# Delta-rule scan of a two-block model: raw key products of a chunk made once for both directions, with a new operation order on four engines

## The reference, cut to what matters

```
kb = k * beta;  gamma = exp(G_i - G_j) below the diagonal
a_low = strict_lower(kb k^T * gamma)          # per chunk and direction
(u, w) = (1 + a_low)^-1 [v*beta, kb*exp(G)]
qk = (q k^T) * gamma
v_new = u - w s;  o = (q exp(G)) s + qk v_new;  s = s exp(G_last) + (k exp(G_last - G))^T v_new
```

## Time and profile before

| | |
|---|---|
| median of 3 runs | 3566.6 us (3563.71 to 3573.29) |
| the profiled execution, its own time | 3574.62 us |
| its span, first to last instruction | 3572.8 us |
| PE busy, share of the span | 3451.9 us, 97% |
| DVE, ACT, POOL busy | 61%, 27%, 13% |
| scan stage, first and second half of the heads | from 1580.5 and from 1919.7 us, some 209 us each |

### The profile page before, as it was taken

One profiled execution on the slowest core, in us unless ns is written; L12 is line 12 of the kernel. 1 busy time (PEld: TensorE's weight loads), 2 busy tenths in 40 slices (PEclk: granted clock), 3 DMA queues, 4 the chain that ended last, 5 costly groups with the idle time before them and its releaser, 6 DMA issues.

```text
span 3572.8 us, 59170 instructions
## 1 busy us (share of the span) xinstructions
PE 3451.9 (97%) x24990; PEld 2877.7 (81%) x24990; DVE 2172.1 (61%) x3040; ACT 980.9 (27%) x1835; POOL 473.9 (13%) x400
## 2 busy tenths in 40 slices
PE   8999999999999999999999999999999999999998
PEld 6777887877778888879887887799988786668887
DVE  4655777646557776655565556854475653864347
ACT  1243101222430012433343322443322203720011
POOL 0000000000000000015402440034440001502000
PEclk9999999999999999999999999999999999999999
DMA  4311444323015443210010013032252331022222
GB/s 173 111 37 48 185 189 176 137 100 112 25 50 207 188 166 125 104 37 3 3 65 25 3 48 125 36 114 100 106 194 71 104 116 48 1 72 104 95 95 95
DMA packets 58055, 338.93 MB, mean 95 GB/s; under 512 B 7580, under 2 KB 8092, under 8 KB 23240
## 3 DMA queue, kind: packets, MB, share of 16 engines
q1 hardware_dynamic: 30492, 220.50, 16.9%
q10 hardware_dynamic: 27308, 114.71, 8.8%
HBM read 309.64 MB, written 18.21 MB: 92 GB/s over the span
## 4 chain that ended last, share of the span: by engine, by line
PE 76%; DVE 8%; PEld 6%; DMA 3%; issue 3%; ACT 2%; PEldq 1%; POOL 0%; POOLq 0%; ACTq 0%; DVEq 0%; another core or an unknown queue 0%; SPq 0%
PE psum L567 19%; PE psum L569 18%; PE psum L568 18%; PE psum L2650 4%; PE psum L2657 4%; DMA pieces_in<-pieces 2%; PEld psum L567 2%; PEld psum L569 2%; PEld psum L568 2%; PE psum L1412 1%; PE psum L1396 1%; PE psum L1385 1%; PE psum L2789 1%; PEldq L507 1%; PE psum L4234 1%
## 5 line engine op out<-in xcount | busy, mean ns | idle before, releaser
L569 PE MATMUL psum<-xt_operands,pieces_lo 128*128 128x512 f32 (+1 forms) x2016 | 748.9, 371 | 0.0
L567 PE MATMUL psum<-xt_operands,pieces_hi 128*128 128x512 f32 (+1 forms) x1840 | 700.2, 381 | 16.3 <-DVE xt_operands L826 7.0
L568 PE MATMUL psum<-xt_operands,pieces_hi 128*128 128x512 f32 (+1 forms) x1840 | 689.7, 375 | 0.0
L567 PE MATMUL psum<-pieces_hi,xt_operands 128*128 128x512 f32 x1276 | 508.9, 399 | 18.5 <-DVE pieces_lo L616 9.4
L568 PE MATMUL psum<-pieces_lo,xt_operands 128*128 128x512 f32 x1320 | 517.6, 392 | 0.0
L569 PE MATMUL psum<-pieces_hi,xt_operands 128*128 128x512 f32 x1276 | 500.6, 392 | 0.0
L569 PEld LDWEIGHTS psum<-xt_operands,pieces_lo 128*128 128x128 f32 x2016 | 379.6, 188 | 62.7
L567 PEld LDWEIGHTS psum<-xt_operands,pieces_hi 128*128 128x128 f32 x1840 | 346.9, 189 | 87.6 <-issue 13.6
L568 PEld LDWEIGHTS psum<-xt_operands,pieces_hi 128*128 128x128 f32 x1840 | 347.2, 189 | 59.2
L583 DVE CAST pieces_hi<-pieces_in 128x2048 fp32r<-128x2048 f32 x165 | 208.2, 1262 | 254.5 <-DMA pieces_in<-pieces 125.2
L567 PEld LDWEIGHTS psum<-pieces_hi,xt_operands 128*128 128x128 f32 x1276 | 242.3, 190 | 76.4 <-DVE pieces_lo L616 10.5
(11 more groups left out here) (464 smaller groups left out, 5586.6 us busy)
## 6 DMA issues: line engine op xcount, KB each, us to landing
pieces_in<-pieces SPq DMA_DIRECT2D x210, 1024.0 KB, 4.9
x_mem<-ada ACTq DMA_DIRECT2D x28, 1024.0 KB, 4.8
arena<-ada ACTq DMA_DIRECT2D x20, 1024.0 KB, 4.8
hid<-arena ACTq DMA_DIRECT2D x22, 384.0 KB, 4.4
arena<-mods ACTq DMA_DIRECT2D x10, 512.0 KB, 17.0
arena<-hid ACTq DMA_DIRECT2D x3, 1536.0 KB, 11.6
arena<-arena ACTq DMA_DIRECT2D x32, 128.0 KB, 4.4
arena<-hid ACTq DMA_DIRECT2D x1, 3840.0 KB, 16.2
```

The costliest lines, as they stand in the source:

```text
L567: signal_later(k, pe.matmul(out, sh, mh, start=start, stop=False, skip_group_check=reopened))
L568: signal_later(k, pe.matmul(out, sh, ml, start=False, stop=False, skip_group_check=reopened))
L569: return pe.matmul(out, sl, mh, start=False, stop=stop, skip_group_check=reopened)
```

## The change

Raw products are made once. `kk` and `qk` run only at the first visit of a chunk (`first_visit`). There DVE reads them from PSUM as before, and ACT then copies them to SBUF (new `kkc`, `qkc`, 128x512 each) into places that are free at that time (`kept`): parts of `oacc`, of kT and qT, and of k and v for the context chunks. At the second visit DVE's `low0` and `qg` read the kept copy, so that both of their inputs are in SBUF.

The bank of a raw product comes free only when ACT has copied it. `oa` of a first visit is a copy in place of an addition, so that `oacc` is no longer cleared; the two clears of the state no longer wait for one another.

All four orders are new, and PE and DVE work on steps t-1 and t-2 (`LAG` is 2, one more turn of the loop). Several waits that followed from the old order are written out (among them `dup` before the next `diff`, `-xx1`, `-wy`); where the order of signals implies them, no wait is issued.

```diff
+def first_visit(s, d):
+    return CHUNKS[d][s] not in CHUNKS[1 - d][:s]
+def kept(k, name, s, d):
+    c, q = CHUNKS[d][s], int(name == "qk")
+    if c >= NT1:
+        return k.oacc[:, 2 * (c - NT1) + q, :, :]
+    if c in (0, 3):
+        return (k.kT if c == 0 else k.qT)[:, :, P * (NT1 + q):P * (NT1 + q) + P]
+    return (k.kc_ if c == 1 else k.vc_)[:, NT1 + q, :, :]
...
-TAKEN = dict(gb="diff", kk="low0", qk="qg", ...
+TAKEN = dict(gb="diff", kk="kkc", qk="qkc", ...
...
     def kk(s, d):
+        if not runs(s) or not first_visit(s, d):
+            return
         product(s, d, "kk", chunk(k.kT), chunk(k.kT))
...
-    for t in range(N_STEPS + 1):
-        a3(t - 1, 0); x4(t - 1, 0); a1(t - 1, 1); x8(t - 1, 0); ks(t - 1, 1); wy(t - 1, 0); x2(t - 1, 1)
-        a2(t - 1, 1); qk(t - 1, 1); xx0(t - 1, 0); a3(t - 1, 1); z0(t - 1, 0); x4(t - 1, 1); y1(t - 1, 0)
-        o1(t - 1, 1); x8(t - 1, 1); xx1(t - 1, 0); gb(t, 0); wy(t - 1, 1); w2(t - 1, 0); y2(t - 1, 0); gb(t, 1)
-        xx0(t - 1, 1); xx2(t - 1, 0); z0(t - 1, 1); y1(t - 1, 1); vn(t - 1, 0); xx1(t - 1, 1); o1(t - 1, 0)
-        w2(t - 1, 1); y2(t - 1, 1); o2(t - 1, 0); xx2(t - 1, 1); su(t - 1, 0); vn(t - 1, 1); kk(t, 0)
-        o2(t - 1, 1); qk(t, 0); kk(t, 1); ul(t, 0); su(t - 1, 1); a1(t, 0); ks(t, 0); a2(t, 0); x2(t, 0)
-        ul(t, 1)
+    for t in range(N_STEPS + LAG):
+        ul(t - 2, 0); gb(t - 1, 0); ks(t - 2, 1); a1(t - 2, 0); ul(t - 2, 1); x2(t - 2, 0); a2(t - 2, 0)
+        a1(t - 2, 1); a3(t - 2, 0); x4(t - 2, 0); a2(t - 2, 1); x2(t - 2, 1); x8(t - 2, 0); a3(t - 2, 1)
+        x4(t - 2, 1); wy(t - 2, 0); x8(t - 2, 1); xx0(t - 2, 0); z0(t - 2, 0); wy(t - 2, 1); y1(t - 2, 0)
+        o1(t - 2, 0); xx0(t - 2, 1); xx1(t - 2, 0); o1(t - 2, 1); y1(t - 2, 1); z0(t - 2, 1); w2(t - 2, 0)
+        y2(t - 2, 0); xx1(t - 2, 1); gb(t - 1, 1); xx2(t - 2, 0); y2(t - 2, 1); w2(t - 2, 1); vn(t - 2, 0)
+        xx2(t - 2, 1); qk(t - 1, 0); o2(t - 2, 0); vn(t - 2, 1); qk(t - 2, 1); su(t - 2, 0); o2(t - 2, 1)
+        su(t - 2, 1); kk(t - 1, 0); ks(t - 1, 0); kk(t - 1, 1)
...
+    def keep(s, d, name, src, done):
+        if runs(s) and first_visit(s, d):
+            st.begin(name, s, d, (done,))
+            st.done(act.activation(kept(k, src, s, d), bank(k, src, s, d), ACT.Copy))
...
+    for t in range(N_STEPS + LAG):
+        l4c(t - 1, 0); l2c(t - 1, 1); l8c(t - 1, 0); l4c(t - 1, 1); l8c(t - 1, 1); xf(t - 1, 0); y1c(t - 1,
+        0); z0c(t - 1, 0); gamt(t - 1, 1); xf(t - 1, 1); v1c(t - 1, 0); y1c(t - 1, 1); z0c(t - 1, 1); w2c(t
+        - 1, 0); y2c(t - 1, 0); v1c(t - 1, 1); y2c(t - 1, 1); w2c(t - 1, 1); vnc(t - 1, 0); vnc(t - 1, 1)
+        gamt(t, 0); qkc(t - 1, 1); gam(t, 0); qkc(t, 0); gam(t, 1); kkc(t, 0); l2c(t, 0); kkc(t, 1)
...
     def low0(s, d):
         t = k.buf[d]["t"]
-        tt(s, d, "low0", t, ps("kk", s, d), t, ALU.mult, "gam", "kk")
+        if runs(s):
+            tt(s, d, "low0", t, shared(s, d, "kk", "kkc"), t, ALU.mult, "gam")
...
+    for t in range(N_STEPS + LAG):
+        lvm(t - 2, 0); ulm(t - 2, 1); diff(t - 1, 0); r1(t - 2, 1); lvm(t - 2, 1); x2a(t - 2, 0); rr(t - 2,
+        0); x4a(t - 2, 0); x2a(t - 2, 1); x8a(t - 2, 0); x4a(t - 2, 1); wya(t - 2, 0); x8a(t - 2, 1); wya(t
+        - 2, 1); t1(t - 2, 0); rr(t - 2, 1); t1(t - 2, 1); diff(t - 1, 1); v2a(t - 2, 0); v2a(t - 2, 1)
+        t2(t - 2, 0); qg(t - 2, 1); s2(t - 2, 0); qg(t - 1, 0); low0(t - 1, 0); low(t - 1, 0); t2(t - 2, 1)
+        s2(t - 2, 1); ulm(t - 1, 0); low0(t - 1, 1); low(t - 1, 1); r1(t - 1, 0)
...
-    e.link(pool.memset(k.oacc, 0.0))
...
+            if first_visit(s, d):
+                st.begin("oa", s, d, ("t2",))
+                st.done(pool.tensor_copy(o, k.buf[d]["tb"]))
...
+    for t in range(N_STEPS + LAG):
+        kd(t - 1, 1); s1(t - 1, 0); s1(t - 1, 1); dup(t, 0); dlow(t, 0); dup(t, 1); dlow(t, 1); oa(t - 1,
+        0); x1(t, 0); oa(t - 1, 1); bv(t, 0); kd(t, 0); x1(t, 1); bv(t, 1)
```

More of the change, by code:

```diff
@@ L2501 @@
 ORDERS = {
[L2502 to L2506, removed]
@@ L2507 @@
-    "act": order("y1c.0' v1c.0' w2c.0' y2c.0' xf.1' z0c.1' y1c.1' v1c.1' vnc.0' w2c.1' y2c.1' gamt.0 vnc.1' gam.0 "
-      "gam.1 l2c.0 l4c.0 l8c.0 gamt.1 l2c.1 l4c.1 xf.0 l8c.1 z0c.0 "),
-    "pool": order("x1.1' kd.0' s1.1' s1.0' dup.0 dlow.0 oa.0' dup.1 dlow.1 x1.0 kd.1 bv.1 bv.0 oa.1' "),
-}
+    "pe": order("ul.0'' gb.0' ks.1'' a1.0'' ul.1'' x2.0'' a2.0'' a1.1'' a3.0'' x4.0'' a2.1'' x2.1'' x8.0'' a3.1'' "
+      "x4.1'' wy.0'' x8.1'' xx0.0'' z0.0'' wy.1'' y1.0'' o1.0'' xx0.1'' xx1.0'' o1.1'' y1.1'' z0.1'' w2.0'' "
+      "y2.0'' xx1.1'' gb.1' xx2.0'' y2.1'' w2.1'' vn.0'' xx2.1'' qk.0' o2.0'' vn.1'' qk.1'' su.0'' o2.1'' "
+      "su.1'' kk.0' ks.0' kk.1' "),
@@ new lines @@
+    "dve": order("lvm.0'' ulm.1'' diff.0' r1.1'' lvm.1'' x2a.0'' rr.0'' x4a.0'' x2a.1'' x8a.0'' x4a.1'' wya.0'' "
+      "x8a.1'' wya.1'' t1.0'' rr.1'' t1.1'' diff.1' v2a.0'' v2a.1'' t2.0'' qg.1'' s2.0'' qg.0' low0.0' "
+      "low.0' t2.1'' s2.1'' ulm.0' low0.1' low.1' r1.0' "),
+    "act": order("l4c.0' l2c.1' l8c.0' l4c.1' l8c.1' xf.0' y1c.0' z0c.0' gamt.1' xf.1' v1c.0' y1c.1' z0c.1' w2c.0' "
+      "y2c.0' v1c.1' y2c.1' w2c.1' vnc.0' vnc.1' gamt.0 qkc.1' gam.0 qkc.0 gam.1 kkc.0 l2c.0 kkc.1 "),
@@ new lines, with first_of, exists @@
+    "pool": order("kd.1' s1.0' s1.1' dup.0 dlow.0 dup.1 dlow.1 oa.0' x1.0 oa.1' bv.0 kd.0 x1.1 bv.1 "),
+}
+def first_visit(s, d):
+    return CHUNKS[d][s] not in CHUNKS[1 - d][:s]
+def first_of(s, d):
+    return CHUNKS[1 - d].index(CHUNKS[d][s]), 1 - d
+def exists(name, s, d):
+    return name not in ("kk", "qk", "kkc", "qkc") or first_visit(s, d)
+def kept(k, name, s, d):
[5 more added lines that the diff above has]
+    return (k.kc_ if c == 1 else k.vc_)[:, NT1 + q, :, :]
@@ L2517, in counted @@
         n = 0
-        for turn in range(steps + 1):
+        for turn in range(steps + LAG):
             for name, d, back in ops:
-                if 0 <= turn - back < steps:
+                if 0 <= turn - back < steps and exists(name, turn - back, d):
                     n += 1
@@ L2527 @@
 PE_AT = {n: key for key, (engine, n) in AT.items() if engine == "pe"}
-TAKEN = dict(gb="diff", kk="low0", qk="qg", ul="lvm", a1="l2c", x2="x2a", a2="l4c", x4="x4a", a3="l8c", x8="x8a", wy="wya", xx0="xf", z0="z0c", y1="y1c", xx1="v1c", w2="w2c", y2="y2c", xx2="v2a", ks="r1", vn="vnc", o1="t1", o2="t2", su="s2")
+TAKEN = dict(gb="diff", kk="kkc", qk="qkc", ul="lvm", a1="l2c", x2="x2a", a2="l4c", x4="x4a", a3="l8c", x8="x8a", wy="wya", xx0="xf", z0="z0c", y1="y1c", xx1="v1c", w2="w2c", y2="y2c", xx2="v2a", ks="r1", vn="vnc", o1="t1", o2="t2", su="s2")
 IN_BLOCKS = ("xx0",)
@@ L2546 @@
 PLACE = rings()
+CORNERS = [key[1:] for _, key in sorted(PE_AT.items()) if key[0] == "xx2"]
+CORNER_AHEAD = dict(zip(CORNERS[1:], CORNERS))
 class Steps:
@@ L2637, in ready @@
             pe.wait_ge(k.S.padding_ready, 1)
+        if name in ("ks", "o1") and s == 0:
+            pe.wait_ge(k.S.padding_ready, 2 + d)
         st.begin(name, s, d, needs)
@@ L2902, in vnc @@
     def vnc(s, d):
[L2903 to L2909, removed]
+        copy(s, d, "vnc", "vn", "vn", "vn", "-o2", "-su")
+    for t in range(N_STEPS + LAG):
[3 more added lines that the diff above has]
+        gamt(t, 0); qkc(t - 1, 1); gam(t, 0); qkc(t, 0); gam(t, 1); kkc(t, 0); l2c(t, 0); kkc(t, 1)
     for d in range(2):
@@ L3038, in dlow @@
         t = k.buf[d]["t"]
-        tt(s, d, "dlow", t, t, heads(gmask[:, d, :]), ALU.add, "dup")
+        tt(s, d, "dlow", t, t, heads(gmask[:, d, :]), ALU.add, "diff", "dup")
     def dup(s, d):
```

89 lines of the change are left out of this document (49 added, 40 removed).

## The result

The changed kernel takes 3613.81 us (median of 4, 3612.72 to 3625.62) against 3568.27 for the one before in the same session (3563.71 to 3573.29): ratio 1.0135, 95% interval 1.0109 to 1.016. The forecast was 3527 us with a range of 3510 to 3550. It had the sign wrong, and the time is beyond every rival, the slow one (3590) too.

A forecast was written before the change was run, and what follows sets the result against it. PE's summed instruction work was taken to bound the scan. A, B and C save 27.2 us per half, D costs 7.6, leaving 39.2 in both: 3566.6 - 39.2 = 3527.4 us, range 3510 to 3550.

The forecast's parts named there:

- the slow one (3590): R4, the rival in which waits at ul lose the clock: 3590 us, chance 0.05.
- A: PE's raw products: six kk and six qk removed from each half, saving 10.9 us a half.
- B: PE's changes of tile size: 17 a turn instead of 31, saving 14.3 us over six turns.
- C: Scan's start and end: clears no longer chained, last o2 not waiting for ACT; saves 0.3 and 1.7 us.
- D: New PE stalls: 5.5 us at ul of direction 0, 2.1 at other hops; 7.6 us per half.
- R4: PE's waits at ul lose the clock: 2 + 4.5 us each turn, 3590 us; chance 0.05.

The follow-up runs named there:

- after_spare: Changed kernel plus 8 spare 128x256 matmuls, results unread, ahead of z0 of direction 0 in every visit: 3583.5 us, ratio 1.0047.
- order_spare: order_only plus 8 spare 128x256 matmuls, results unread, ahead of z0 of direction 0 in every visit: 3580.33 us, ratio 1.0035.
- share_only: Kernel before with its old orders, plus only the sharing of raw products and ACT's copies kkc and qkc: 3566.52 us, ratio 1.0002.
- qk_only: Kernel before in its old order, with only qk (not kk) shared, 96 products fewer: 3564.43 us, ratio 0.9993.
- before_spare: Kernel before plus 8 spare 128x256 matmuls, results unread, at z0 of direction 0 in every visit: 3608.64 us, ratio 1.0119.
- the burst: Kernel before plus 640 independent 32x32 matmuls at the start of each scan: 3636.2 us (one run) against 3566.2.
- order_only: Changed kernel's new orders without the sharing, every raw product made at each visit, no copies: 3580.53 us, ratio 1.0035.
- after_spare_ul: Changed kernel plus 4 spare 128x256 matmuls in the wait ahead of ul of direction 0: 3590.15 us, ratio 1.0062.
- late_qg_o1_spare2: Changed kernel with direction 0's qg behind low and qk behind kk, both o1 among the small blocks, 2 spare matmuls at z0: 3633.68 us, ratio 1.0185.

## Why the prediction was wrong, step by step

| both halves, us | forecast | measured |
|---|---|---|
| A, products | -21.8 | -16.6 |
| B and C, changes of size, start and end | -32.6 | -25.0 |
| D, waits at ul | +11.0 | +12.0 |
| D, other data waits | +4.2 | +1.5 |
| pauses in the supply | none | +28.8 |
| clock | none | +50.9 |
| sum | -39.2 | +51.6 (scans: +43.1) |

Where the measured ones are from: A is after_spare less order_spare (+2.2 us in the scans' 441.8 and 439.6), less the waits at ul (12.0), the clock (5.2) and the pauses (1.6) that come with it. share_only has PE 16.2 us less busy, which agrees; qk_only has 10.7 for half of the products, which gives the forecast's price. B and C are order_spare less before_spare (439.6 - 466.7 = -27.1), without 4.4 of clock loss that went and with 2.3 of pauses that came. The rows overlap by 8.5 us, which stays unassigned; I have no run that divides it. Each row comes from single profiled runs, and the runs of one kernel differ by several us (after_spare from 3577 to 3592), so a row is rough to that extent.

**The step that failed** is in the first part: "So what a steady turn costs is the sum of PE's instructions, and the change must be priced as PE work first, and then for new waits." The sum had two kinds of time, work and data waits. The order before had only three pauses of 0.2 us, its 32x32 blocks standing between 64x64 blocks and products, and gathering blocks of one size, which is where B's gain came from, also gathered the shortest instructions. The xx0 of the earlier trace rows, 32 matmuls in 0.38 us, is 64 instructions; 256 such instructions take 1.5 us, and the burst shows them arriving every 3.5 to 4.0. The trace of before had the warning, and the prediction did not use it. In the steady turn of the earlier trace rows it has a transfer of instructions every 3.6 to 4.3 us from 1728.89 to 1749.11, close to the pace at which the burst starves; three of the six:

```profile
1733.00:1733.40 0.40, 0.40 (x4) 0.40 (x5) 0.40 (x2) 0.13 (x1) 0.40 (x1) 1.00 0.16 41
1736.60:1737.00 0.40, 0.40 (x6) 0.40 (x6) 0.25 (x1) 0.31 (x1) 0.00 (x0) 1.00 0.22 41
1741.00:1741.40 0.40, 0.40 (x18) 0.33 (x14) 0.00 (x0) 0.00 (x0) 0.40 (x1) 1.00 0.20 41
```

The three pauses named "issue" in its second scan were a sign as well. The second thing that the sum put at nothing, the clock, is the larger: 50.9 us.

**A and B** were right in kind and count (192 records; the fewer changes of size gain, order_spare against before_spare), and together with C too large: 54.4 forecast, 41.6 measured. **C**: the wait for ACT before the last o2 is gone, and the first ul waits 4.20 instead of 5.26 us. **D** at ul came out near in its sum, 12.0 against 11.0, by the mechanism that the forecast named, and partly by luck: three turns a half wait 2.0 us (forecast 1.5, with one operation held up where two are), and the two others, forecast at 0.5 each, don't wait. The Trainium skill's "SBUF — State Buffer", section "Who interferes with whom", has the later of the two operations blocked, and low's 1.64 beside POOL's 1.59 us agrees.

**R4** had the clock as a mechanism, at 0.05, with 2 us of stall and 4.5 us of clock in each turn. Measured over twelve turns are 3.4 us of stall (pauses and waits at ul) and 4.2 us of clock a turn, so its mechanism was real and its price of a fall was near; it lacked the pauses. It was held unlikely because the one fall that it knew came with a gap of 5.26 us, and in these runs the clock fell with pauses of 2 us and behind three short waits in a row. Its "against" was the clock of 1.00 in the steady turns of a kernel that had no gaps in them, which says nothing of one that has.

**And the sharing:** even with the pauses cured, after_spare is no faster than order_spare (+2.2 us in the scans), and share_only no faster than before. What the products give back, data waits take, in either order. With the pauses left in, it is worse: the kernel after is 33 us slower than order_only (3613.8 against 3580.5), although it does less work. Its profile has 12.0 us more of waits at ul, 4.9 of pauses and 22.1 of clock loss. **Left open** is how the clock loss divides between pauses and waits at ul: the two together lose 61.8 us; with only the waits it is 12.3 (after_spare), with only the pauses 39.7 (order_only), or 35.9 (after_spare_ul, most of the wait filled); with next to nothing of either it is 7.1 (order_spare) and 10.9 (before). So the pauses carry the larger part, and the wait adds to it where both come in one turn.

## What to carry to other kernels

An engine that is busy all the time has a second limit beside its work: the rate at which instructions reach it. Before small matmuls are gathered, count instructions in the densest stretch and set them against the slowest supply that a trace shows; long instructions between them are not only a cost. And price a stall on TensorE at more than its length: here 29 us of pauses and 12 us of waits brought 51 us of clock loss, so work that is "free of waits" on paper with margins of 0.1 us should be forecast with that price. When PE work is taken out of a turn, ask first whether the chain over the other engines is shorter than what is left.

## What the runs showed of the hardware

- Instructions of TensorE arrived 256 at a time, 3.5 to 4.0 us apart in a row of 32x32 matmuls, while 128 of these took 1.3 us at the full clock and 1.93 at half of it; 148 matmuls ran before the first pause in one scan and 196 in the other. The pauses of the burst, the kernel after and order_only, 54 in all, ended 2.2 to 3.0 us after the start of a 16 KB transfer.
- Added work made a kernel faster: 4 spare matmuls a visit (half of 43.1 us, 21.5) left it 41 us faster on the whole.
- In the kernel after the granted clock fell to 0.50 with pauses of 2 us and came back 3 to 17 us later; in late_qg_o1_spare2 it fell after 3 us in which PE was busy for 1.7. In those 17 us a product (eight records of 128x128) took up to 2.08 us for 1.16.
- An operation of VectorE with both inputs in SBUF took 1.64 and 1.76 us where GpSimd's had begun before it, and 0.69 where it began 0.02 us ahead.
